# Two LayerNorms in halves, a decay by Exp, and the queue order of a decode block

## The reference

```python
x = layer_norm(x, ln_in_g, ln_in_b)                        # 1024 features
xa, ga, xb, gb, gc, q, k, v, xp = split(x @ w_in, 9)       # 9 groups of 256
# mixer A
xc = causal_conv(xa, width 4); r = sigmoid(xc @ wa + ba); i = sigmoid(xc @ wx + bx)
log_a = -8 * r * softplus(-lambda); a = exp(log_a)
b = sqrt(-expm1(2 * log_a)) * (i * xc); h[t] = a[t] * h[t-1] + b[t]; ya = h * gelu(ga)
# mixers B (short convolution), C (stick-breaking attention), D (causal pooling)
x = layer_norm(ALPHA * x + concat(ya, yb, yc, yd) @ w_out, ln1_g, ln1_b)
x = layer_norm(ALPHA * x + square(relu(x @ w_ff1)) @ w_ff2, ln2_g, ln2_b)
```

## Time and profile before

| | us |
|---|---|
| median of 3 runs (2698.26 to 2709.3) | 2707.09 |
| the profiled execution | 2702.74 |
| its span | 2700.9 |
| TensorE busy, matmul (share of the span) | 2522.9 (93%) |
| VectorE busy | 1559.2 (58%) |
| ScalarE busy | 1272.5 (47%) |
| GpSimd busy | 123.6 (5%) |
| mean granted clock of TensorE | 0.967 |

### The profile page before, as it was taken

How to read it: one execution, slowest core, us unless ns; L and a number is a source line. 1 busy time by engine, 2 the same in 40 slices (tenths; PEclk the granted TensorE clock), 3 DMA queues, 4 the chain that set the end, 5 groups by cost and what they waited for, 6 DMA issues and landing times.

```text
span 2700.9 us, 37244 instructions
## 1 busy us (share of the span) xinstructions
PE 2522.9 (93%) x13647; PEld 2414.8 (89%) x13647; DVE 1559.2 (58%) x2235; ACT 1272.5 (47%) x1968; POOL 123.6 (5%) x271
## 2 busy tenths in 40 slices
PE   4899999768999999999999999999898989999997
PEld 4898899758999999999999999999877978999996
DVE  5445753164676766777765776746544644574434
ACT  4444511253565564565564565544344444354331
POOL 0001220000000000000100000000000000000000
PEclk9999999958999999999999999999899989999998
DMA  5433453232343443443443443333455455343332
GB/s 180 135 121 112 130 161 105 92 107 79 113 142 112 129 123 96 141 133 106 134 118 102 138 132 110 114 122 104 127 167 180 149 168 178 109 129 115 117 117 72
DMA packets 147886, 339.08 MB, mean 126 GB/s; under 512 B 19977, under 2 KB 79882, under 8 KB 147578
## 3 DMA queue, kind: packets, MB, share of 16 engines
q1 hardware_dynamic: 141498, 317.08, 38.4%
q0 software_dynamic: 6208, 19.63, 2.4%
HBM read 291.72 MB, written 44.92 MB: 125 GB/s over the span
## 4 chain that ended last, share of the span: by engine, by line
PE 73%; issue 8%; SPq 8%; DVE 5%; ACT 3%; DMA 2%; POOL 1%; DVEq 0%; ACTq 0%; POOLq 0%
PE PS L943 18%; PE PS L944 18%; PE PS L945 18%; SPq L628 4%; SPq L623 4%; PE PS L702 3%; PE PS L703 3%; PE PS L704 3%; PE PS L767 2%; PE PS L754 1%; PE PS L789 1%; PE PS L788 1%; PE PS L755 1%; PE PS L954 1%; DMA rows_a<-x_all 1%
## 5 line engine op out<-in xcount | busy, mean ns | idle before, releaser
L1205 ACT ACTIVATE w_hi<-w_raw 128x1024 fp32r<-128x1024 f32 x238 | 250.5, 1053 | 289.9 <-PE PS L945 286.8
L943 PE MATMUL PS<-a_hi,w_hi 128*128 128x416 f32 x1048 | 377.0, 360 | 5.7 <-DVE a_lo L1733 5.7
L944 PE MATMUL PS<-a_lo,w_hi 128*128 128x416 f32 x1048 | 370.3, 353 | 0.0
L945 PE MATMUL PS<-a_hi,w_lo 128*128 128x416 f32 x1048 | 369.5, 353 | 0.0
L1702 DVE TENSOR_TENSOR w_lo<-w_raw,w_hi 128x1024 fp32r<-128x1024 f32 x238 | 290.2, 1219 | 82.4 <-ACT w_hi L1205 82.0
L943 PE MATMUL PS<-h_hi,w_hi 128*128 128x416 f32 x872 | 316.2, 363 | 3.9 <-DVE h_lo L1727 3.9
L944 PE MATMUL PS<-h_lo,w_hi 128*128 128x416 f32 x872 | 309.0, 354 | 0.0
L945 PE MATMUL PS<-h_hi,w_lo 128*128 128x416 f32 x872 | 308.6, 354 | 0.0
L1727 DVE TENSOR_TENSOR h_lo<-h_full,h_hi 128x416 fp32r<-128x416 f32 x160 | 94.5, 591 | 230.5 <-ACT h_hi L1218 230.3
L943 PEld LDWEIGHTS PS<-a_hi,w_hi 128*128 128x128 f32 x1048 | 200.4, 191 | 10.0 <-issue 6.2
L1205 ACT ACTIVATE w_hi_c<-w_raw 128x1024 fp32r<-128x1024 f32 x120 | 126.3, 1053 | 160.1 <-PE PS L945 152.0
(11 more groups left out here) (263 smaller groups left out, 5070.4 us busy)
## 6 DMA issues: line engine op xcount, KB each, us to landing
w_raw<-w_all SPq DMA_DIRECT2D x378, 512.0 KB, 3.7
pages<-ck SPq DMA_DIRECT2D x128, 128.0 KB, 2.1
pages<-cv SPq DMA_DIRECT2D x128, 128.0 KB, 2.1
proj_scratch<-stage SPq DMA_DIRECT2D x70, 208.0 KB, 2.1
k_rows<-kv_out SPq DMA_DIRECT2D x80, 128.0 KB, 4.1
x_scratch<-x_full SPq DMA_DIRECT2D x20, 416.0 KB, 2.5
x_residual<-x_scratch SPq DMA_DIRECT2D x5, 1664.0 KB, 9.0
y_out<-nat SPq DMA_DIRECT2D x20, 416.0 KB
```

Source lines behind the costliest of these rows:

```text
L943: pe.matmul(out, w_h, mh_[:, k, :], start=(g == 0), stop=False)
L944: pe.matmul(out, w_h, ml_[:, k, :], start=False, stop=False)
L945: ins = pe.matmul(out, w_l, mh_[:, k, :], start=False, stop=(g == KT - 1))
L1205: act.activation(w_hi(n), raw[:, n % 2, :], ACT.Copy).then_inc(s_wh, 1)
```

## The change

1. **Halves.** For block 0's first LayerNorm and the last block's second one, the first 512 features are transposed three steps earlier (n = KT - 3 and N_STEPS - 3) into PSUM banks 4 to 7, one for each row group; ScalarE copies them to `nat3`, VectorE takes their statistics. After the last step the second halves follow into the same banks (`second_half`), each once ScalarE's copy of the first is made. Statistics, square root and reciprocal are then made for four row groups at once. Block 0: VectorE normalises the first halves in `nat3`, ScalarE the second ones. Last block: VectorE makes the first halves with gain and bias; ScalarE normalises the second halves, GpSimd multiplies by the gain, VectorE adds the bias; the stores are eight half rows.
2. **Decay.** ScalarE makes it with Exp from the sigmoid (scale -8 softplus) ahead of Tanh; the reciprocal, +1 and 2t-1 go from VectorE. The product goes to `a_gate` in place of `a_t`; `a_load(n)` waits for the landed store of piece n - 2.
3. **VectorE's order** in the projection stage: `split_lo` last in a step.
4. **Block 3.** SP issues pages ahead of `load_weights(n + 4)`; x1 is loaded at r = 28. `sample_new` goes in three parts at r = 5, 7 and 8; TensorE waits for its 8 differences by count. `sample_pairs` goes to the middle of the step.

```diff
@@ SP
             for n in range(N_STEPS):
+                b, r = divmod(n - KT, STEPS_B)
+                if b == 3:
+                    if r == 9:
+                        for u in range(RING):
+                            sample_pages(u)
+                    for u in range(RING, SUNITS):
+                        if r == (K_AT + (u - RING) // 2 if u < 32 + RING else V_AT + (u - 36) // 2):
+                            sample_pages(u)
                 if n + 4 < N_STEPS:
                     load_weights(n + 4)
...
-                    if r == 20:
+                    if r == (20 if b < 3 else 28):
                         load_x1(b + 1)
...
+            for half, made, n in ((0, s_row, (NB - 1) * NR), (1, s_row2, 0)):
+                for j in range(NR):
+                    at = (NB - 1) * BLK + j * ROW
+                    sp.wait_ge(made, n + j + 1)
+                    sp.dma_start(y_out[at:at + ROW, half * 512:half * 512 + 512], nat3[0:ROW, j, half * 512:half * 512 + 512]).then_inc(s_out, 16)
@@ PE
-                if half == 0 and r - V_AT >= 3 and (r - V_AT - 3) % 2 == 0 and (r - V_AT - 3) // 2 < DECB:
+                if half == 1 and r - V_AT >= 3 and (r - V_AT - 3) % 2 == 0 and (r - V_AT - 3) // 2 < DECB:
...
+            def first_half(src):
+                for j in range(NR):
+                    for k in range(4):
+                        ins = pe.transpose(PS[0:ROW, 4 + j, k * P:(k + 1) * P], src[:, k, j * ROW:(j + 1) * ROW], ident[:, :])
+                    ins.then_inc(s_fh, 1)
...
+                if n == KT - 3:
+                    attention_paused(ALONE)
+                    pe.wait_ge(s_oev, 4)
+                    first_half(xr)
                 if n == KT:
-                    attention_paused(ALONE)
-                    for j in range(NR):
-                        norm1_row(0, j)
+                    pe.wait_ge(s_oev, KT)
+                    second_half(xr, 0)
                     norm1_back(0, range(KT))
+                if n == N_STEPS - 3:
+                    pe.wait_ge(s_fev, NB * FT - 4)
+                    first_half(acc)
@@ ACT
+                act.activation(at[:, :], ar[:, :], ACT.Exp, scale=lam[:, c, 2:3])
                 own.op(act.activation(ar[:, :], ar[:, :], ACT.Tanh, scale=lam[:, c, 7:8]))
...
+            def half_copies(done):
+                for j in range(NR):
+                    act.wait_ge(s_fh, done + j + 1)
+                    act.activation(nat3[0:ROW, j, 0:512], PS[0:ROW, 4 + j, :], ACT.Copy).then_inc(s_fc, 1)
+            def half_norms(e, n1):
+                act.wait_ge(s_ve, NB + e + NR)
+                act.activation(std[0:ROW, :], var[0:ROW, :], ACT.Sqrt).then_inc(s_std, NR)
+                act.wait_ge(s_nmr, NB + n1 + NR)
+                for j in range(NR):
+                    norm(PS[0:ROW, 4 + j, :], nat3[0:ROW, j, 512:D], j, j)
@@ DVE, a_rest
                 dve.wait_ge(s_aact, n + 1)
-                if n:
-                    dve.wait_ge(s_mst[0], 16 * n)
-                op(dve.tensor_scalar(at[:, :], ar[:, :], 1.0, None, ALU.add))
-                op(dve.reciprocal(at[:, :], at[:, :]))
                 own.up(dve.tensor_tensor(ai[:, :], ai[:, :], axc[:, n % 2, :], ALU.mult))
-                own.up(dve.tensor_scalar(ar[:, :], at[:, :], 2.0, -1.0, ALU.mult, ALU.add))
-                op(dve.scalar_tensor_tensor(out=aq[:, :], in0=aq[:, :], scalar=2.0, in1=at[:, :], op0=ALU.mult, op1=ALU.mult))
+                op(dve.scalar_tensor_tensor(out=aq[:, :], in0=at[:, :], scalar=1.0, in1=aq[:, :], op0=ALU.add, op1=ALU.mult))
...
-                if b == NB - 1:
-                    split_lo(p + 2)
                 if j in A_AT:
                     a_conv(A_AT[j])
...
+                if b == NB - 1:
+                    split_lo(p + 2)
...
+            def half_stats(done):
+                for j in range(NR):
+                    dve.wait_ge(s_fc, done + j + 1)
+                    own.up(dve.bn_stats(bn[0:ROW, j, 0, :], nat3[0:ROW, j, 0:512]))
...
+            def norm1_halves():
+                half_rstd(0)
+                half_nmr(0)
+                for j in range(NR):
+                    row = nat3[0:ROW, j, 0:512]
+                    dve.tensor_scalar(row, row, rstd[0:ROW, j:j + 1], nmr[0:ROW, j:j + 1], ALU.mult, ALU.add).then_inc(s_natd, 1)
+            def norm2_halves():
+                half_rstd(NR * (2 * NB - 1))
+                half_nmr(NB * NR)
+                for js in ((0, 1), (2, 3)):
+                    for j in js:
+                        row = nat3[0:ROW, j, 0:512]
+                        own.up(dve.scalar_tensor_tensor(out=row, in0=row, scalar=mv[0:ROW, j, 0:1], in1=gb2[0:ROW, 0, 0:512],
+                                                        op0=ALU.subtract, op1=ALU.mult))
+                    own.sync()
+                    for j in js:
+                        row = nat3[0:ROW, j, 0:512]
+                        dve.scalar_tensor_tensor(out=row, in0=row, scalar=rstd[0:ROW, j:j + 1], in1=gb2[0:ROW, 1, 0:512],
+                                                 op0=ALU.mult, op1=ALU.add).then_inc(s_row, 1)
+                for j in range(NR):
+                    row = nat3[0:ROW, j, 512:D]
+                    dve.wait_ge(s_gain, j + 1)
+                    dve.tensor_tensor(row, row, gb2[0:ROW, 1, 512:D], ALU.add).then_inc(s_row2, 1)
...
-                if r == K_AT - 3:
-                    sample_new()
+                if r in (K_AT - 5, K_AT - 3, K_AT - 2):
+                    sample_new((K_AT - 5, K_AT - 3, K_AT - 2).index(r))
@@ POOL, a_load and the end
                 if n >= 2:
-                    pool.wait_ge(s_amade, n - 1)
+                    pool.wait_ge(s_mst[0], 16 * (n - 1))
...
+            for j in range(NR):
+                row = nat3[0:ROW, j, 512:D]
+                pool.wait_ge(s_nat, NATB + NB * NR + j + 1)
+                pool.tensor_tensor(row, row, gb2[0:ROW, 0, 512:D], ALU.mult).then_inc(s_gain, 1)
```

More of the change, by code:

```diff
@@ L662, in _ @@
                         sample_inputs()
[L663 to L668, removed]
                     if r == 51:
@@ L818, in sample_new @@
                 ins.then_inc(s_vnt, 1)
-                pe.wait_ge(s_qw, 1)
+                pe.wait_ge(s_qw, 2 * NH)
                 pe.wait_ge(s_kn, 1)
@@ L955, in forward, with second_half @@
                 ins.then_inc(s_ft, 1)
+            def first_half(src):
[3 more added lines that the diff above has]
+                    ins.then_inc(s_fh, 1)
+            def second_half(src, done):
+                for j in range(NR):
+                    pe.wait_ge(s_fc, done + j + 1)
+                    for k in range(4):
+                        ins = pe.transpose(PS[0:ROW, 4 + j, k * P:(k + 1) * P], src[:, 4 + k, j * ROW:(j + 1) * ROW], ident[:, :])
+                    ins.then_inc(s_ft, 1)
             def norm1_row(b, j):
@@ L1014, in _ @@
                 dense(n)
-            for j in range(NR):
-                norm2_row(NB - 1, j)
+            pe.wait_ge(s_fev, NB * FT)
+            second_half(acc, NR)
         @block.scalar
@@ L1376, in _ @@
                         norm2_std(b - 1, ROWS2.index(r))
-            for j in range(NR):
-                norm2_std(NB - 1, j)
+            half_norms(NR * (2 * NB - 1), NB * NR)
         @block.vector
@@ new lines, in half_nmr @@
+            def half_nmr(n1):
+                dve.scalar_tensor_tensor(out=nmr[0:ROW, :], in0=mv[0:ROW, :, 0], scalar=-1.0, in1=rstd[0:ROW, :], op0=ALU.mult,
+                                         op1=ALU.mult).then_inc(s_nmr, NR)
+                dve.wait_ge(s_nmr, NB + n1 + NR)
+            def norm1_halves():
+                half_rstd(0)
+                half_nmr(0)
+                for j in range(NR):
+                    row = nat3[0:ROW, j, 0:512]
+                    dve.tensor_scalar(row, row, rstd[0:ROW, j:j + 1], nmr[0:ROW, j:j + 1], ALU.mult, ALU.add).then_inc(s_natd, 1)
@@ L1785, in norm2_row, with sample_new @@
                                          op1=ALU.add).then_inc(s_row, 1)
-            def sample_new():
-                dve.wait_ge(s_kqs, 96)
-                op(dve.memset(qw[:, :].bitcast(F32), 0.0))
+            def sample_new(part):
+                if part == 0:
+                    dve.wait_ge(s_kqs, 96)
+                    op(dve.memset(qw[:, :].bitcast(F32), 0.0))
                 def window(half, h, part):
@@ L1935, in _ @@
                         norm2_row(b - 1, ROWS2.index(r))
-            for j in range(NR):
-                norm2_row(NB - 1, j)
+            norm2_halves()
         @block.gpsimd
@@ L2047, in _ @@
                     pool.tensor_copy(nP[:, t % 6, w:w + 1], nP[:, (t - 4) % 6, 0:1]).then_inc(s_car, 1)
+            pool.wait_ge(s_gb, 16)
+            for j in range(NR):
+                row = nat3[0:ROW, j, 512:D]
+                pool.wait_ge(s_nat, NATB + NB * NR + j + 1)
+                pool.tensor_tensor(row, row, gb2[0:ROW, 0, 512:D], ALU.mult).then_inc(s_gain, 1)
 def _tiles(w, rows, cols):
```

74 lines of the change are left out of this document (48 added, 26 removed).

## The result

| | before | after |
|---|---|---|
| median, us | 2706.27 (4 runs) | 2665.63 (4 runs, 2661.48 to 2668.67) |
| profiled execution, its span | 2702.74, 2700.9 | 2661.48, 2659.8 |
| mean granted clock | 0.967 | 0.977 |

The ratio is 0.9853, interval 0.9827 to 0.988: 1.5% faster. The kernel was timed again later beside other experiments, 2665.39 against 2706.71.

What follows compares the result with a forecast made beforehand. TensorE was taken as the bound, losing time standing still and at 1.2 GHz afterwards. Terms -16 - 5.3 - 13.7 - 6.6 = -41.6 us from the 2707.09 median gave 2665.5, forecast 2666; own range 2658 to 2674, wider range 2646 to 2689.

Steps and rivals of the forecast that it cites:

- mixing stage: Projections with mixer A beside them: a shorter mixer turn removes TensorE's idle time and half clock, 16 us gained.
- block 0's LayerNorm: LayerNorm after the out projection: back transposes start 7.2 us earlier, less 1.9 for transposes moved ahead, net -5.3 us.
- block 3: Block 3's key and value phases: earlier pages and shorter waits, partly given back at step 29, net -13.7 us.
- the end: Last LayerNorm and products: last addition 8.5 us earlier, less 1.9 for transposes moved ahead, net -6.6 us.
- about 0.45 for the gate matmuls: Projection stage: gate matmuls add about 0.45 us to TensorE's three steps of 13.6, making 14.05 us per mixer turn.
- Bound 18.6: Projection stage, 228 to 380 us: most that could be gained, 13.5 us idle plus 5.1 at half clock.
- Rival 1: Projection stage hardly gains, as store landing and table load cancel the reciprocal's saving: 4 us instead of 16, 2678; chance 0.17.
- square root 0.25: Block 0's first LayerNorm: the square root after the variance takes 0.25 us before the reciprocal.
- Step (e): Block 3's value phase: value loads and pages wait for pages_lo(32) instead of step 33's w_lo, -4.9 us.
- (f): Block 3's value phase: pairs at half step remove y-row waits from step fronts; only the last unit's tail counts, -1 us.
- VectorE's eight half rows (0.61 each and two waits): Last LayerNorm: VectorE's half-row operations at 0.61 us each, with two waits, finish 10.2 us after the first transpose.
- I take 1.3 each: Last LayerNorm: GpSimd's multiplications of the second halves take 1.3 us each, finishing 11.0 us after the first transpose.

Runs made afterwards that it cites:

- best_b: Changed kernel with step 29's weight tile ahead of the pages, block 0's Sqrt before its wait, and end products on VectorE after ScalarE's normalisation, without GpSimd: 2655.12 us.

## Why the prediction was right, and where its terms were not

2666 was forecast, 2665.63 measured. The terms, against the two traces that were compared first:

| term | forecast | measured |
|---|---|---|
| mixing stage | -16 | -20.8 |
| block 0's LayerNorm | -5.3 | -4.0 |
| block 3 | -13.7 | -15.6 (in the means -11.5) |
| the end | -6.6 | -2.2 |
| start and attention alone | none | +1.5 |
| sum | -41.6 | -41.2 |

The mechanisms were right in the main; that the sum came out to 0.4 us is luck. The mixing stage gave 4.8 more, the end 4.4 less, and block 3's 15.6 holds some 4 us of scatter.

**Mixing stage, mis-sized.** The turn worked out came out at 13.05, forecast 14. TensorE's own pace was too short in the sum: "about 0.45 for the gate matmuls" gave 14.05, and three steps without a wait take 15.0 in both kernels. So the ring had some 1 us in hand and not "almost nothing". Bound 18.6 was passed: it counted the idle time in 228 to 380, and TensorE had waited 1.0 us before 228 as well; the last 1.2 us stay open. I had argued the move of `split_lo` at nothing, as cover; by itself it is worth 11.4. Rival 1 fell: the landing took 2 us of a turn as forecast, and the convolution starts 3.7 us after its load is issued, where it was 6.5. I had put that delay down to b loads ahead; GpSimd's rows of the kernel before have them behind:

```profile
277.13 0.54 POOL L1972 DMA_DIRECT2D a_x<-proj_scratch  x1
...
281.46 0.54 POOL L1996 DMA_DIRECT2D b_x<-proj_scratch  x1
```

What held the loads there, no run tells. The Trainium skill, "ScalarE: Activation LUTs", section "Table sets: the hidden batching unit", has Exp in another set than Sigmoid, and the trace agrees: ten loads more, 1283 ns each. The 2.66 us that the Trainium skill gives for a switch (same page, section "What ACT_TABLE_LOAD costs") showed nowhere: the next ACTIVATE follows a load at once, and ahead of the ten new loads ScalarE is idle for 0.2 us in all. It waits 68.8 us for TensorE in this window, so the added time is off the path.

**Block 0.** 7.2 earlier was forecast, 5.7 came. The step that failed is "square root 0.25": the table load, hidden ahead of the wait in the kernel before, here came behind it, 1.28. Another 0.5 went into the back transposes, 5.18 us where they were 4.68. The first halves' cost in step 4 of the out projection (1.65 against 1.9) was right.

**Block 3.** Signs and sizes by stretch: step 12 10.5 earlier in the means where 11.5 was forecast; x1 3.4 against 3.5; the stand ahead of step 29, 8.3 us in the trace, gives back 8.0 against 7.2. Step (e) was right: unit 36's pages come 4.8 sooner after the start of step 30, 4.9 forecast, with the stand and without. But the division before it was wrong: the start is as much the windows' as the queue's, and x1's 3.5 does not add to the stand's 7.2 but is taken out of it. So step 30 starts only 4.6 earlier in the means (8.4 in the first two traces) where 7.8 was forecast. Steps 30 to 39 gave 6.8 where (e) and (f) had 5.9; the pairs were not undone alone.

**The end, the step that failed.** "VectorE's eight half rows (0.61 each and two waits)": alone they take 0.75, and four of them 1.57 to 1.75 beside GpSimd, 3.8 us more. "I take 1.3 each" for GpSimd was right for an undisturbed multiplication (1.27); beside these rows it took 1.61 to 1.71. The last product came 16.8 us after the first transpose, at the bound of 16.6, where 12.7 was forecast. The Trainium skill, "GPSIMD Engine Reference", section "Specifications", names this contention for VectorE operations with two SBUF inputs; I had cited it with up to 4 us and left it out of the sum. The trace agrees: the last product came 4.1 us later than forecast, nearly all of it VectorE's slowed rows. I gave no price to two engines at work together, which no row before showed. On top of that the end comes 4.1 us after the last store's issue, 3.6 in the kernel before. GpSimd's share should have been left on VectorE.

## What to carry over

A ring over several engines and an in-order queue can each hold the same late work: undo both and one at a time before giving the gain to either. An engine's help is to be priced with both engines at work; in the changed kernel the multiplications handed to GpSimd slowed VectorE by 3.8 us and ended its work 0.6 later than doing them itself. Where a queue's order is changed for a phase, look at the last item of the phase: one weight tile behind the last pages gave back 8 us, and one tile moved ahead of them brought 6.2 of them back to the block. And one trace is not enough for a stretch that scatters: block 3's 15.6 us were 11.5 in the means.

## What the runs showed of the hardware

- VectorE's 104x512 `scalar_tensor_tensor` with two SBUF inputs: 0.75 us alone, 1.57 to 1.75 beside a whole GpSimd `tensor_tensor` of the same size, which then takes 1.61 to 1.71 itself. With one input in PSUM VectorE takes 0.74 beside it, and GpSimd 1.27.
- A Sqrt's table load ran ahead of the wait in the kernel before and behind it in the changed one, with the wait written in the same way. Why, no run tells; an activation without a wait ahead of it settles the place.
- Eight half-row stores: where the last six are issued 0.6 us apart, the span ends 4.1 us after the last issue; where they go in pairs, one pair 2.0 us or more after the other (VectorE alone, `best_b`), 2.8. So 1.3 us at the end go with the crowding; that the crowding causes them was not tested alone.
- In the stand of 8.3 us ahead of step 29 the granted clock fell to 1.2 GHz, from 2071.1 to 2077.9. In the value phase, with stands of up to 2.0 us, it stayed at 2.4; before, with stands of up to 2.2 there, it fell six times.
